# Wide high products in the even layer, with the gated output on GpSimd and ScalarE

## What is computed

```
p = rms_norm(x) @ even_w_in                 # 2048 -> 3 * 1024 + 3232 columns
qa, ka, va = split(p[..., :3072], 3)        # differential attention, 8 heads
q, k = partial_rope(qa), partial_rope(ka)
w = softmax(q1 k1 / 8) - lam * softmax(q2 k2 / 8);  o = w @ v;  rms_norm(o) * 0.2
# the other columns: RWKV-7 mixing, 16 heads of 64
xm = p + (previous token of p - p) * mu;  r, k, v, wl, al, gl = split(xm)
# per token: state = state * w + (state @ -kk) (kk * a) + v k;  y = state @ r
b_out = (group_norm(y) + (sum(r * k * r_k) * v)) * (sigmoid(gl) @ g_up)
x = x + concat(a_out, b_out) @ even_w_out
x = x + (silu(h @ w_gate) * (h @ w_up)) @ w_down,  h = rms_norm(x)
```

## Time and profile before

| | |
|---|---|
| median of 3 runs | 2507.18 us (2506.55 to 2507.42) |
| profiled execution | 2504.34 us, of which the span is 2502.5 us |
| even layer: prologue | 0 to 60 us of the span |
| even layer: steps 0 to 6 | 60 to 418 us, 51.2 us each |
| even layer: step 7 | 418 to 468 us |
| PE busy | 2474.1 us, 99% of the span |
| granted TensorE clock | 0.999 of full speed on average |

### The profile page before, as it was taken

One profiled execution on the slowest core, in us unless ns is written; L12 is line 12 of the kernel. 1 busy time (PEld: TensorE's weight loads), 2 busy tenths in 40 slices (PEclk: granted clock), 3 DMA queues, 4 the chain that ended last, 5 costly groups with the idle time before them and its releaser, 6 DMA issues.

```text
span 2502.5 us, 47792 instructions
## 1 busy us (share of the span) xinstructions
PE 2474.1 (99%) x17536; PEld 2187.6 (87%) x17536; DVE 1852.5 (74%) x3043; ACT 1224.1 (49%) x1753; POOL 490.9 (20%) x407
## 2 busy tenths in 40 slices
PE   8999999999999999999999999999999999999998
PEld 8899998888888888888888888888888888888887
DVE  7898889776665666566989999997666556655665
ACT  6555565554433444334656565655444434443444
POOL 1222222122200221022212212113222012200220
PEclk9999999999999999999999999999999999999999
DMA  7333332445555555555554444446455555555553
GB/s 272 117 126 134 124 121 108 164 180 190 186 194 191 184 184 196 190 185 179 178 203 163 168 157 175 154 154 222 179 185 186 200 187 185 198 192 185 194 191 128
DMA packets 65576, 438.43 MB, mean 175 GB/s; under 512 B 9408, under 2 KB 10816, under 8 KB 15808
## 3 DMA queue, kind: packets, MB, share of 16 engines
q1 hardware_dynamic: 61632, 436.29, 48.6%
q10 hardware_dynamic: 3840, 0.70, 0.1%
HBM read 434.87 MB, written 2.10 MB: 175 GB/s over the span
## 4 chain that ended last, share of the span: by engine, by line
PE 83%; DVE 8%; issue 4%; ACT 3%; POOL 1%; DMA 0%; ACTq 0%; DVEq 0%; SPq 0%; POOLq 0%
PE acc L332 24%; PE acc L402 17%; PE mixer_banks L413 9%; PE acc L384 9%; PE acc L396 9%; PE acc L367 5%; PE acc L329 5%; DVE w_low L322 2%; DVE arena L1534 2%; ACT L955 1%; DVE arena L445 1%; DVE arena L1522 1%; POOL arena L607 1%; DVE arena L1524 1%; PE mixer_banks L1656 1%
## 5 line engine op out<-in xcount | busy, mean ns | idle before, releaser
L317 ACT ACTIVATE w_high<-w_raw 128x1024 fp32r<-128x1024 f32 x831 | 862.5, 1057 | 871.7 <-PE acc L384 388.6
L322 DVE TENSOR_TENSOR w_low<-w_raw,w_high 128x1024 fp32r<-128x1024 f32 x832 | 1055.8, 1296 | 119.8 <-ACT w_high L317 117.3
L332 PE MATMUL acc<-h_split,w_high 128*128 128x512 f32 x2688 | 670.9, 393 | 1.1
L332 PEld LDWEIGHTS acc<-h_split,w_high 128*128 128x128 f32 x2688 | 491.7, 188 | 99.4 <-DVE arena L445 3.1
L562 POOL TENSOR_TENSOR arena<-arena,norm_scale 128x256 f32<-128x256 f32 x152 | 224.5, 1477 | 1355.7 <-DVE arena L445 1336.0
L445 DVE TENSOR_REDUCE arena<-acc 128x256 f32<-128x512 f32 x254 | 174.7, 688 | 288.0 <-PE acc L402 178.2
L402 PE MATMUL acc<-h_split,w_high 128*128 128x512 f32 x1376 | 328.2, 391 | 0.0
L402 PEld LDWEIGHTS acc<-h_split,w_high 128*128 128x128 f32 x1376 | 252.9, 188 | 48.9
L367 PE MATMUL acc<-h_split,w_low 128*128 128x256 f32 x1824 | 274.9, 282 | 0.0
L367 PEld LDWEIGHTS acc<-h_split,w_low 128*128 128x128 f32 x1824 | 255.5, 190 | 15.1
L332 PE MATMUL acc<-mix_split,w_high 128*128 128x512 f32 x752 | 185.1, 393 | 2.6 <-DVE mix_split L1147 2.3
(11 more groups left out here) (322 smaller groups left out, 2415.1 us busy)
## 6 DMA issues: line engine op xcount, KB each, us to landing
w_raw<-w_gu SPq DMA_DIRECT2D x176, 1024.0 KB, 4.8
w_raw<-w_odd SPq DMA_DIRECT2D x64, 1024.0 KB, 4.7
w_raw<-w_even SPq DMA_DIRECT2D x49, 1024.0 KB, 4.8
w_raw<-w_last SPq DMA_DIRECT2D x44, 1024.0 KB, 4.8
w_raw<-w_down SPq DMA_DIRECT2D x32, 1024.0 KB, 4.9
w_raw<-w_down SPq DMA_DIRECT2D x16, 768.0 KB, 4.2
w_raw<-w_odd_out SPq DMA_DIRECT2D x12, 1024.0 KB, 4.8
w_raw<-w_even_out SPq DMA_DIRECT2D x10, 1024.0 KB, 4.8
```

The costliest lines, as they stand in the source:

```text
L317: act.activation(wh[:, self.res, ks], raw[:, self.raw, ks], ACT.Copy).then_inc(high_done, 1)
L322: dve.tensor_tensor(wl[:, self.res, ks], raw[:, self.raw, ks], wh[:, self.res, ks].bitcast(F32), ALU.subtract).then_inc(low_done, 1)
L332: pe.matmul(acc[self.acc][:, 0:2 * T], wh[:, self.res, k], flat(both), start=k == 0, stop=stop)
```

## The change

- Blocks 2 to 5 of steps 0 to 6 and blocks `EVEN + 3` to `EVEN + 5` of the prologue become wide: 31 blocks of 16 tiles, 496 tiles. Their evacuation becomes the reduction over 512 columns.
- The scaling that this evacuation did is done elsewhere: for v of the mixer by widening `shifts` from 512 to 768 columns; for q and k by multiplying the cosine and sine tables by `nrs` once, in the prologue; for v of the attention by a scale for each token, `nrt`, on ACT's copy, which is split in two. Three DVE instructions in the prologue make the tables and `nrt`.
- `gated` and `rounded` for j = 0 to 6 leave DVE. POOL has `output(j)`: an addition, a multiplication, and the subtraction that makes the low part; ACT's `output_rounded(j)` makes the high part. They stand in step j + 1. In step 7 `gated(7)` and `rounded(7)` stay on DVE.
- DVE's `level(5)` stands ahead of `evacuate(3)` in steps 0 to 6.
- ACT's exponentials of the attention wait for a third `at_mx` instead of `at_nb`; it is the same instruction that raises it.

```diff
         def even_block(j, i=None):
 
             if j == NRW - 1:
-                return lambda u: Block(EVEN_OUT + u, kt=KT - 2 if u >= 0 else KT, narrow=u < 0)
-            return lambda u: Block(EVEN + 6 * j + 6 + u, i, 12, narrow=u not in (0, 1))
+                return lambda u: Block(EVEN_OUT + u, kt=KT - 2 if u >= 0 else KT)
+            return lambda u: Block(EVEN + 6 * j + 6 + u, i, 12)
...
+            def output(j):
+
+                waits(pool, j + 1, "rw_yTs", "rw_bv")
+                pool.tensor_tensor(yT, yT, bv, ALU.add).then_inc(S["rw_out"], 1)
+                pool.wait_ge(S["rw_out"], 2 * j + 1)
+                pool.wait_ge(S["rw_gs"], j + 1)
+                pool.tensor_tensor(yT, yT, gT, ALU.mult).then_inc(S["rw_out"], 1)
+                pool.wait_ge(S["rw_out"], 2 * j + 2)
+                pool.wait_ge(S["rw_rounded"], j + 1)
...
+                pool.tensor_tensor(rest, yT, rounded.bitcast(F32), ALU.subtract).then_inc(S["rw_end"], 1)
...
                 low_part(rn)
-                turn(j, 1)
+                if more:
+                    turn(j, 1)
+                if not isinstance(j, int) or j > 0:
+                    output(j - 1)
+                if not more:
+                    turn(j, 1)
...
+            def output_rounded(j):
+
+                act.wait_ge(S["rw_out"], 2 * j + 2)
+                act.activation(mh[:, NRW + j], yT, ACT.Copy).then_inc(S["rw_rounded"], 1)
...
                 if j > 0:
                     late_loads(j)
+                if j > 0 and not more:
+                    output_rounded(j - 1)
                 high(3)
+                if j > 0 and more:
+                    output_rounded(j - 1)
                 high(4)
...
-                act.activation(flat(avn), bank(4)[:, 0:256], ACT.Copy).then_inc(S["at_vn"], 1)
+                if j == 0:
+                    act.wait_ge(S["dve_once"], 16)
+                for c in range(2):
+                    act.activation(avn[:, c], bank(4)[:, c * P:(c + 1) * P], ACT.Copy, scale=nrt[:, c:c + 1]).then_inc(S["at_vn"], 1)
...
-                    dve.tensor_tensor(r3[:, 0:2, 1:], r3[:, 0:2, 1:], bc(nrs, 2), ALU.mult).then_inc(S["rw_scaled"], 1)
+                    dve.tensor_tensor(r3[:, :, 1:], r3[:, :, 1:], bc(nrs, 3), ALU.mult).then_inc(S["rw_scaled"], 1)
...
                 evacuate(-1)
                 if j == 0:
                     low(2)
-                if not more:
-                    gated(j - 1)
-                    rounded(j - 1)
...
                 if more:
                     low(10)
+                    level(5)
                     evacuate(3)
-                    level(5)
...
                     swap(j + 1, 0)
-                    if j > 0:
-                        gated(j - 1)
...
-                if more and j > 0:
-                    rounded(j - 1)
...
+            tables = cst[:, C_COS:C_COS + 2 * T].rearrange("p (a t) -> p a t", a=2)
+            dve.tensor_tensor(tables, tables, bc(nrs, 2), ALU.mult).then_inc(S["dve_once"], 1)
+            diagonal = otmp.rearrange("p (c t) -> p c t", c=2)
+            dve.tensor_tensor(diagonal, nrs.rearrange("p (c t) -> p c t", c=2), bc(ident, 2), ALU.mult).then_inc(S["dve_once"], 1)
+            dve.wait_ge(S["dve_once"], 15)
+            dve.reduce_sum(nrt, diagonal, AX.X).then_inc(S["dve_once"], 1)
             for u in range(2, 5):
                 Block(EVEN + u + 2).low(dve, 0)
-                Block(EVEN + u, narrow=True).evacuate(dve, even_dst[u])
+                Block(EVEN + u, narrow=u < 3).evacuate(dve, even_dst[u])
...
             for n in range(LOWRANK + 1, EVEN + 6):
-                Block(n, narrow=True).products(pe, 0, hs)
+                Block(n, narrow=n < EVEN + 3).products(pe, 0, hs)
```

More of the change, by code:

```diff
@@ L252, in build @@
         ars = small[:, 56:58]
+        nrt = small[:, 28:30]
         upper = small[:, 48:52]
@@ L281, in build @@
             "rw_S rw_S0 rw_R1 rw_nR1 rw_U1 rw_Us1 rw_y rw_ymean rw_yc rw_ysq rw_yvar rw_yln rw_yrs rw_yn rw_yT rw_yTs",
-            "rw_g rw_gs rw_out rw_end rw_scaled",
-            "at_rot at_sin at_cos at_qk at_s at_sm at_mx at_nb at_p at_rc at_w at_wT at_wt at_vT at_vn at_o at_ss at_ln",
+            "rw_g rw_gs rw_rounded rw_out rw_end rw_scaled",
+            "at_rot at_sin at_cos at_qk at_s at_sm at_mx at_p at_rc at_w at_wT at_wt at_vT at_vn at_o at_ss at_ln",
             "at_rs at_on at_oT at_out at_end",
@@ L575, in low_part @@
                 pool.tensor_tensor(parts[:, 1], whole, parts[:, 0].bitcast(F32), ALU.subtract).then_inc(S["rw_suml"], 1)
+            def output(j):
[6 more added lines that the diff above has]
+                pool.wait_ge(S["rw_rounded"], j + 1)
+                rounded = mh[:, NRW + j] if isinstance(j, int) else mh[:, bass.ds(j + NRW, 1)].rearrange("p a t -> p (a t)")
+                rest = ml[:, NRW + j] if isinstance(j, int) else ml[:, bass.ds(j + NRW, 1)].rearrange("p a t -> p (a t)")
+                pool.tensor_tensor(rest, yT, rounded.bitcast(F32), ALU.subtract).then_inc(S["rw_end"], 1)
             def turn(j, c):
@@ L630, in _ @@
             pool.wait_ge(S["consts_in"], 16)
+            pool.wait_ge(S["dve_once"], 14)
             even_step(0)
@@ L764, in even_step @@
                 z_copy(2)
-                act.wait_ge(S["at_nb"], j + 1)
+                act.wait_ge(S["at_mx"], 3 * j + 3)
                 for q, cols in enumerate((slice(0, P), slice(P, 3 * P))):
@@ L1137, in gated @@
                 dve.tensor_tensor(yT, yT, bv, ALU.add).then_inc(S["rw_out"], 1)
-                dve.wait_ge(S["rw_out"], 3 * j + 1)
+                dve.wait_ge(S["rw_out"], 2 * j + 1)
                 dve.wait_ge(S["rw_gs"], j + 1)
@@ L1142, in rounded @@
             def rounded(j):
-                dve.wait_ge(S["rw_out"], 3 * j + 2)
+                dve.wait_ge(S["rw_out"], 2 * j + 2)
                 dve.tensor_scalar(mh[:, NRW + j], otmp, 1.0, None, ALU.mult).then_inc(S["rw_out"], 1)
-                dve.wait_ge(S["rw_out"], 3 * j + 3)
+                dve.wait_ge(S["rw_out"], 2 * j + 3)
                 dve.tensor_tensor(ml[:, NRW + j], otmp, mh[:, NRW + j].bitcast(F32), ALU.subtract).then_inc(S["rw_end"], 1)
@@ L1270, in even_step @@
                 dve.reduce_max(amx[:, 2:4], prob[:, :, P:3 * P], AX.X).then_inc(S["at_mx"], 1)
-                dve.wait_ge(S["at_mx"], 2 * j + 2)
-                dve.tensor_scalar(anb, amx, -0.125, None, ALU.mult).then_inc(S["at_nb"], 1)
+                dve.wait_ge(S["at_mx"], 3 * j + 2)
+                dve.tensor_scalar(anb, amx, -0.125, None, ALU.mult).then_inc(S["at_mx"], 1)
                 def bonus_factors():
@@ L1343, in even_step @@
                 dve.wait_ge(S["rw_bonus"], j + 1)
+                if j > 0:
+                    dve.wait_ge(S["rw_out"], 2 * j)
                 dve.tensor_tensor(bv, bank(0)[:, 0:T], xm[:, 2], ALU.mult).then_inc(S["rw_bv"], 1)
-                if more and j > 0:
-                    rounded(j - 1)
                 dve.wait_ge(S["rw_ysq"], j + 1)
@@ L1668, in _ @@
                     pe.matmul(bank(0)[:, 0:T], ones, nss, start=True, stop=True).then_inc(S["sq_total"], 1)
-                Block(n, narrow=True).products(pe, 1, hs)
+                Block(n, narrow=n < EVEN + 3).products(pe, 1, hs)
             def even_step(j, block, more=True):
@@ L1796, in even_step @@
                 txt(4)
-                waits(pe, j + 1, "at_wt", "at_vn")
+                pe.wait_ge(S["at_wt"], j + 1)
+                pe.wait_ge(S["at_vn"], 2 * j + 2)
                 pe.matmul(bank(5)[:, 0:P], wt[:, 0:P], avn[:, 0], start=True, stop=True)
```

## The result

| | before | after |
|---|---|---|
| median of 12 runs each, on one chip | 2506.57 us (2503.95 to 2507.42) | 2512.50 us (2510.28 to 2513.31) |
| ratio after / before, 95% interval | | 1.0023 [1.0016, 1.0031] |
| profiled execution, its span | 2504.34, 2502.5 us | 2512.57, 2510.8 us |
| steps 1 to 6, each | 51.21 us | 51.72 us |
| step 0 | 51.21 us | 50.96 us |

The changed kernel is slower by 5.9 us, and the interval of the ratio lies clear of 1. The page's row of engines, next to the earlier trace rows: PE issues 496 matmuls fewer and is busy 0.8 us less. DVE has 6 us more, POOL 12 more. None of it says where the time went.

What follows compares the result with a forecast made beforehand. PE's own sequence was taken to bound the kernel. The terms, -3.1 - 0.8 + 0.3 + 2.1 + 1.4 + 1.6 = +1.5 us on 2507.2, gave 2508.7 us, own range 2505 to 2511.5, full range 2503.0 to 2513.5.

Steps and rivals of the forecast that it cites:

- slower rival: Steps 1 to 6: POOL's addition and multiplication delay DVE's lines 1171 to 1175, about 1.2 us a step; 2513.8 us, 14%.
- term 4: Start of steps 1 to 6: added delays exceed 0.35 us of slack by 0.35 a step, +2.1 us (0 to +7).
- term 1: Wide products on PE, seven steps: cheaper tiles, less 0.3 us for the wait at line 1656; -3.1 us (-2 to -5).
- Term 2: Line 1258's copies moved ahead of the evacuation, so PE need not wait: 7 x -0.12 = -0.8 us (0 to -0.8).
- Term 3: Prologue: three new DVE instructions make PE 0.63 us later, wide blocks give back 0.36; +0.3 us (0 to +1).
- (a): Start of steps 1 to 6: the longer evacuation ahead of the step's last `low` adds 0.15 us.
- (b): Start of steps 1 to 6: PE reaches line 1711 about 0.14 us earlier relative to DVE's chain.
- (c): Start of steps 1 to 6: POOL's subtraction slows DVE's lines 1202 to 1208 by 0.4 us; its first two operations are covered.
- the rival in which the gain stands: POOL finds gaps, step 7's clock stays up, tiles give the full 11 ns: 2503.0 us, or 2501.4; 12%.
- Term 5: Step 7: PE's wait ends at 425.95 instead of 424.54, behind ACT's rounding and POOL; +1.4 us (+1.3 to +2).
- Term 6: Behind step 7's longer wait of 3.7 us, PE's clock runs at half rate for 3.2 us: +1.6 us (0 to +1.6).
- wait at the step's start: Sign: PE idle 0.2 to 0.5 us at line 1711's successor, released by DVE's line 1237, steps 1 to 6, not 0.

Runs made afterwards that it cites:

- e1: Changed kernel with the gated output back on DVE, wide products and the rest kept: 2503.71 us, 0.9987 of the kernel before.
- e6: Kernel before with only level(5) put ahead of evacuate(3) in steps 0 to 6: 2505.38 us, 0.9997 of the kernel before.
- e2: Kernel before with only the gated output moved to POOL and ACT: 2511.86 us, 1.0024 of the kernel before.
- e5: Changed kernel with ACT's rounding of j = 6 in step 7 put ahead of its wait for rw_b: 2506.75 us, 1.0001 of the kernel before.
- b_again: The kernel before, unchanged, traced a second time: 2506.57 us, ratio 0.9999.
- e3: Changed kernel with only the gated output of j = 6, in step 7, back on DVE: 2509.72 us, 1.0015 of the kernel before.
- e4: Changed kernel with POOL's output and ACT's rounding moved later within steps 1 to 6: 2505.66 us, 0.9997 of the kernel before.
- e8: Changed kernel with only ACT's rounding and POOL's subtraction moved late in steps 1 to 6: 2508.56 us, 1.001 of the kernel before.
- e7: e1 plus prologue operations ahead of DVE's low_acts wait and five step-7 tiles ahead of PE's rw_end wait: 2499.70 us, 0.9977 of the kernel before.

## Why the prediction was right and wrong

The time fell into the range of 2503.0 to 2513.5: 2512.5 for 2508.7. In part that is luck. It lies above the forecast's own range, which ended at 2511.5, and 75% had been put on a change within 5.0 us where it is 5.9. The range reached so far only for the slower rival, whose 2513.8 even lies above its end.

The forecast's balance of small terms did not hold. The mechanism of that rival, given 14%, came true, with 1.10 us a step where its price was 1.2. The price itself was near by chance: it took a delay of 0.9 us less 0.40 of cover, where the delay was 0.64 and the cover nothing, and it added 0.35 twice, of which only one is term 4's.

**Terms 1 and 2** (-3.1, -0.8): right. Together 0.56 us a step were given, less term 1's part for the wait at line 1656; e1 has 0.55. The wait at line 1656 (1689) did grow, from 1.3 to 1.9 us in seven times, by 0.08 us a step where that part has 0.04. Term 2 alone is e6's 0.12; a half block of the newly wide blocks takes 1.84 us (1.83 was said), and line 1767 follows its low products by 0.45 us, as said.

**Term 3** (+0.3): right. The wait in the prologue went from 0.21 to 0.97, 0.76 longer where 0.63 was worked out, and the stretch became 0.27 us longer. Of the timeline (DVE, then PE), next to the earlier trace rows:

```profile
48.87 0.42 DVE L444 TENSOR_TENSOR arena<-acc,norm_scale 128x256 f32<-128x256 f32 x1
...
49.43 2.08 PE L333 MATMUL acc<-h_split,w_high 128*128 128x512 f32 x8 [0.97 <-DVE arena L444]
```

**Term 4** (+2.1 for six steps, with a range of 0 to +7; measured 6 x 1.10 = +6.6): this is the step that failed. The parts (a) and (b), 0.15 + 0.14, came out at 0.36. Part (c) for the subtraction, 0.4, came out at 0.45. The 0.64 us of the addition and the multiplication were put at nothing. Two readings of the trace led there, and both were wrong. First, the idle 0.40 us ahead of line 1196 was taken for cover. It ends by ACT's line 742, which itself waits for DVE's line 1175, so a delay ahead of line 1175 moves both ends of the idle time; in e2 it was delayed by 0.65 us and the idle time stayed 0.40. The prediction had the condition, "if ACT isn't made late", and did not look whether it holds. The row named its releaser; the reasoning had to follow that releaser one step further back. Second, "the scan at line 1171 overlaps a POOL operation unhurt", said for the rival in which the gain stands, was read from a merged row, 1.13 us for two. The two scans of the kernel before, taken singly (ns, min/median/max, the first alone and then both):

```profile
L1171 DVE TENSOR_TENSOR_SCAN arena<-constants_sb,arena x1: 812/812/812, 164.5 to 164.5; 128x128 f32<-128x128 f32 x1
...
L1171 DVE TENSOR_TENSOR_SCAN arena<-constants_sb,arena x2: 396/604/812, 164.5 to 165.2; 128x128 f32<-128x128 f32 x2
```

The first, under POOL's line 587 (164.28 to 165.02), took 0.81 us; the second, with POOL idle, 0.40. The victim and its price stood in the trace of before. In the changed kernel both take 0.8:

```profile
L1203 DVE TENSOR_TENSOR_SCAN arena<-constants_sb,arena x2: 793/800/808, 166.2 to 166.9; 128x128 f32<-128x128 f32 x2
```

With 0.41 for the second scan and 0.25 for the tiny operation, term 4 would have been 6 x 1.0 and the forecast 2512.7; the 0.41 could be read from the trace of before, the 0.25 shows only in the kernels with the output on POOL.

**Term 5** (+1.4): right. The wait in step 7 is 3.85 us for 2.28, +1.57, released by POOL's line 589 as said. By e5 the wait was a matter of one place in ACT's queue: with the rounding ahead of line 760, where ACT idled 0.65 us, it is 0.3.

**Term 6** (+1.6): a low clock came, but nearly twice as long: 5.9 us of PE's work at 1.2 GHz, about 2.9 us lost (an estimate, half of it). The other error was to take one trace's 1.00 behind a wait of 2.28 us as the kernel's state. By b_again it isn't, and part of the low clock is in the median of before. The other way round, the profiled execution of before lay 2.2 us below its median, 1.5 of it in this stretch. So the difference of the medians, 5.9, is less than that of the traces, 8.3; against the second trace of before (span 2504.8) it is 6.0.

Added up as measured: terms 1 and 2 seven times -0.55 = -3.9, term 3 +0.3, term 4 +6.6, term 5 +1.6, term 6 between +1.2 (against b_again, with its 1.7 by the same estimate) and +2.9, and 0.3 us of stall in step 0, which no term foresaw: +6.1 to +7.8. The medians have +5.9, the two traces +7.5 without the launch.

**The bounds that were to show it.** Steps of over 51.6 us were named as the sign of the slower rival, and they took 51.72; its other sign, line 1175 ending 0.4 us later after the step's start, came with 1.0. In its own words it "decides" there, and by its own bound of 51.6 the prediction is wrong, though its range held. The wait at the step's start was foretold as 0.2 to 0.5 us and is 1.01; in step 0, where none was foretold, it is 0.27.

## What to carry over

Before an idle time is counted as slack, follow its releaser back: if that one waits for an instruction ahead of the delay, the idle time moves along and covers nothing. Work that is moved to GpSimd is priced by which VectorE instructions it will lie beside, each by its own row and never by a merged one, and it goes where nobody waits for VectorE; moved some 20 us later the same three operations cost PE nothing. A long wait of PE is worth removing beyond its own length, since the clock behind it may fall. One trace doesn't tell whether it does: the same kernel showed both.

## What the runs showed of the hardware

**A VectorE operation beside a GpSimd operation waits for its end.** In the rows of step 2 each lengthened DVE operation ends by its own length after POOL's operation has ended, less 0.1 us: line 1234 at 173.59 (POOL's end 173.30 + 0.42 - 0.13), line 1206 at 168.16 (168.14 + 0.17 - 0.15), the first scan at 166.99 (166.70 + 0.40 - 0.11). Line 1167's 0.82 is the same thing: it ends at 164.35, POOL's line 584 at 164.21 (164.21 + 0.29 - 0.15). In step 0 it starts first, takes 0.29, and POOL's line 587 takes 0.87 for its usual 0.74:

```profile
60.95 0.29 DVE L1167 TENSOR_SCALAR arena<-arena 128x256 f32<-128x256 f32 x1 [3.29 <-ACT arena L727]
...
60.98 0.87 POOL L587 TENSOR_TENSOR arena<-arena 128x256 f32<-128x256 f32 x1
```

So a short victim can lose more than its own length: the 0.17 us of a 128x2 operation became 0.42. The Trainium skill, "SBUF — State Buffer", "Who interferes with whom", says that the ports which VectorE and GpSimd share are an exclusive lock: whoever issues first has them for the whole instruction, and the other fully blocks. The trace agrees but for the 0.1 us. By the same section an operation with at most one SBUF input contends only in a 2-port mode; the tiny one-input `TENSOR_SCALAR` was slowed, and no row shows its mode.

**The clock behind a wait is not a property of the wait's length alone.** In step 7 it stayed at 2.4 GHz behind 2.28 us (before, e6) and fell to 1.2 GHz for 3.4 us behind 2.30 (b_again). Behind 2.6 us it was low for 3.4 us in e1 and 6.8 in e3; behind 3.69 for 3.4 (e2); behind 3.85 for 6.8 (after, e4, e8). In e5 and e7, where this wait was 0.3 and 0.8 us, it stayed up. The wait after step 7 is 2.36 us in all eleven traces; behind it the clock was low for 3.4 us in seven and not at all in four (e2, e3, e5, e7). The same stretch of 8 us behind that wait, first of the changed kernel and then of e5:

```profile
478.00:486.00 8.00, 7.34 (x43) 7.09 (x44) 4.99 (x8) 4.60 (x5) 0.31 (x1) 0.79 0.71 249
...
473.00:481.00 8.00, 7.40 (x50) 6.87 (x51) 6.41 (x9) 4.60 (x6) 0.32 (x1) 1.00 0.62 247
```

What decides between these stays open. In b_again 3.4 us at the low level made step 7 1.5 us longer. In the others part of the low time can lie in the wait itself, where it costs nothing; half of what falls on PE's work is 1.7 to 3.1 us a wait in step 7 (an estimate from the seven traces with a low clock there).
